# Routing tokens to experts by a table of token numbers and gates, and adding the experts' rows in DRAM

## The reference, cut to what matters

```python
x = layer_norm(DN_ALPHA * x + merged @ w_out[l], ln1_g[l], ln1_b[l])          # x1
gates = shared_group_router(xt, w_router, b_router)   # 2 of 16 experts, both in one group of 4
for e in range(N_EXPERTS):
    h = jax.nn.silu(xt @ w_gate[e]) * (xt @ w_up[e])                           # 1024 -> 512
    out = out + gates[:, e:e + 1] * (h @ w_down[e])                            # 512 -> 1024
x = layer_norm(DN_ALPHA * x + moe, ln2_g[l], ln2_b[l])
```

## Time and profile before

| what | us |
|---|---|
| median of 3 runs (lowest, highest) | 889.34 (886.75, 891.99) |
| the profiled execution | 887.89 |
| its span, first to last instruction | 886.4 |
| busy PE / DVE / ACT / POOL | 845.4 / 574.0 / 465.1 / 76.0 |
| weights of the experts, 96 loads of 1 MB, to landing (median) | 10.1 to 11.3 |

### The profile page before, as it was taken

How to read it: one execution, slowest core, us unless ns; L and a number is a source line. 1 busy time by engine, 2 the same in 40 slices (tenths; PEclk the granted TensorE clock), 3 DMA queues, 4 the chain that set the end, 5 groups by cost and what they waited for, 6 DMA issues and landing times.

```text
span 886.4 us, 12480 instructions
## 1 busy us (share of the span) xinstructions
PE 845.4 (95%) x4015; PEld 700.4 (79%) x4015; DVE 574.0 (65%) x623; ACT 465.1 (52%) x482; POOL 76.0 (9%) x137
## 2 busy tenths in 40 slices
PE   6999999979999999999999998899999999999993
PEld 5888788868888888888889988688888888888751
DVE  4777444333447884423445589478899889888727
ACT  3555433423466653323226541567787878778610
POOL 1100000400000000000000001301101110010040
PEclk9999999989999999999999998999999999999997
DMA  6565555873233334434329925699999999999753
GB/s 183 165 183 174 166 184 201 244 270 96 82 99 105 95 95 139 146 95 119 94 73 293 286 86 190 248 355 376 381 372 381 383 380 371 380 382 382 274 181 127
DMA packets 168096, 195.85 MB, mean 221 GB/s; under 512 B 7998, under 2 KB 106918, under 8 KB 168070
## 3 DMA queue, kind: packets, MB, share of 16 engines
q1 hardware_dynamic: 154374, 157.69, 53.4%
q0 software_dynamic: 10624, 32.57, 10.8%
q10 hardware_dynamic: 3072, 5.24, 1.6%
HBM read 164.94 MB, written 30.54 MB: 221 GB/s over the span
## 4 chain that ended last, share of the span: by engine, by line
PE 83%; DVE 6%; DMA 6%; ACT 2%; issue 1%; POOL 1%; SPq 0%; ACTq 0%; DVEq 0%; POOLq 0%
PE psA L554 7%; PE psA L553 7%; PE psA L555 7%; PE psA L722 6%; PE psA L723 6%; PE psA L724 6%; PE psB L553 6%; PE psB L555 6%; PE psB L554 6%; PE psB L743 3%; PE psB L745 3%; PE psB L744 3%; DMA wst<-in_w_out_dram 2%; DMA wst<-in_w_in_dram 2%; PE psD L553 2%; PE psD L555 2%
## 5 line engine op out<-in xcount | busy, mean ns | idle before, releaser
L1289 DVE TENSOR_TENSOR elo<-est,ehi 128x2048 fp32r<-128x2048 f32 x94 | 211.3, 2288 | 36.1 <-ACT ehi L971 36.0
L971 ACT ACTIVATE ehi<-est 128x2048 fp32r<-128x2048 f32 x92 | 173.3, 1914 | 35.7 <-DMA est<-in_w_exp_down_dram 14.9
L1102 DVE TENSOR_TENSOR wlo<-wst,whi 128x1024 fp32r<-128x1024 f32 (+1 forms) x78 | 97.5, 1249 | 96.8 <-ACT whi L818 95.7
L818 ACT ACTIVATE whi<-wst 128x1024 fp32r<-128x1024 f32 (+1 forms) x78 | 84.0, 1077 | 92.8 <-PE psA L555 36.4
L722 PE MATMUL psA<-ehi,xe_hi 128*128 128x512 f32 x256 | 101.7, 397 | 1.9 <-DVE xe_lo L1482 1.9
L723 PE MATMUL psA<-elo,xe_hi 128*128 128x512 f32 x256 | 100.5, 392 | 0.0
L724 PE MATMUL psA<-ehi,xe_lo 128*128 128x512 f32 x256 | 100.4, 392 | 0.0
L553 PE MATMUL psB<-xT_hi,whi 128*128 128x512 f32 x208 | 80.9, 389 | 0.0
L554 PE MATMUL psB<-xT_lo,whi 128*128 128x512 f32 x208 | 80.9, 389 | 0.0
L555 PE MATMUL psB<-xT_hi,wlo 128*128 128x512 f32 x208 | 80.9, 389 | 0.0
L722 PEld LDWEIGHTS psA<-ehi,xe_hi 128*128 128x128 f32 x256 | 48.5, 189 | 12.2 <-DVE xe_lo L1482 2.5
(11 more groups left out here) (277 smaller groups left out, 1613.5 us busy)
## 6 DMA issues: line engine op xcount, KB each, us to landing
est<-in_w_exp_gate_dram SPq DMA_DIRECT2D x32, 1024.0 KB, 11.3
est<-in_w_exp_up_dram SPq DMA_DIRECT2D x32, 1024.0 KB, 10.1
est<-in_w_exp_down_dram SPq DMA_DIRECT2D x32, 1024.0 KB, 10.9
wst<-in_w_in_dram SPq DMA_DIRECT2D x60, 512.0 KB, 4.0
xs<-zero POOLq DMA_DIRECT2D x23, 512.0 KB, 3.1
wst<-in_w_out_dram SPq DMA_DIRECT2D x16, 512.0 KB, 5.4
wst<-in_w_branch_r_dram SPq DMA_DIRECT2D x8, 640.0 KB, 4.3
ys<-yb ACTq DMA_DIRECT2D x32, 160.0 KB, 5.1
```

Of the source, the lines that this page charges most:

```text
L818: A(whi[p][:, 0:K, :], wst[p][:, 0:K, :], ACT.Copy).then_inc(w_hi, 1)
L971: A(ehi[s][:], est[s][:], ACT.Copy).then_inc(gu_hi if s < 4 else d_hi, 1)
L1102: V.tensor_tensor(wlo[p][:, 0:K, :], wst[p][:, 0:K, :], whi[p][:, 0:K, :], ALU.subtract).then_inc(w_lo, 1)
L1289: V.tensor_tensor(elo[s][:], est[s][:], ehi[s][:], ALU.subtract).then_inc(gu_lo if s < 4 else d_lo, 1)
```

## The change

The rows are no longer copied to `xs` and `ys`. x1 is stored twice in DRAM: `x1d`, from which the experts' rows are fetched, and `acc`, to which their outputs are added; each has 128 trash rows behind its 512. A table `tab` has for each of the 23 x 128 slots the token number and the gate, divided by alpha; an empty slot has a trash row's number (a different one for each slot of a block) and gate 0.

- SP loads slots 0 and 1 of expert 1, stores x1 to `x1d` tile by tile as it is ready and then to `acc`, and only then loads slots 2 to 5; no load waits for rows any more.
- POOL makes small constants, and after weight tile 20 clears the table and the trash rows, in place of all zero stores.
- The token numbers of blocks 0 and 1 come from DVE comparisons and eight small bf16 matmuls (keys, `chosen_by`, `pick0`), and POOL gathers these two blocks as soon as x1 is stored. Then it scatters the table's 8-byte entries with eight indirect DMAs, loads the whole table to SBUF (`lists`), and gathers block b when block b - 2 is transposed, into two buffers. Numbers of trash rows are out of bounds for a gather and are skipped.
- ACT evacuates the outputs scaled by the table's gates, into two buffers, and issues no DMA. POOL adds all 128 rows of a block to `acc` by an indirect DMA with add, when the add before has landed.
- The gates are computed before `dest` is released; both are in the table.
- In the tail SP loads the four tiles of `acc` when all adds have landed, and the layer norm is taken from them, with epsilon divided by alpha squared. PE has no part in it.
- The turns of PE are unrolled by two, those of ACT completely.

```diff
...
-            for s in range(6):
-                if s == 5:
-                    sp.wait_ge(xe_landed, 32)
+            for s in range(2):
+                load_expert(sp, 1, s)
+            for t in range(TT):
+                sp.wait_ge(x1_done, t + 1)
+                sp.dma_start(x1d[t * P:(t + 1) * P, :], x1[:, t, :]).then_inc(x1_stored, 16)
+            for t in range(TT):
+                sp.dma_start(acc[t * P:(t + 1) * P, :], x1[:, t, :]).then_inc(acc_seeded, 16)
+            for s in range(2, 6):
                 load_expert(sp, 1, s)
...
+            sp.wait_ge(y_stored, (more + NE) * 16)
+            for t in range(TT):
+                sp.dma_start(xa[:, t, :], acc[t * P:(t + 1) * P, :]).then_inc(got[t], 16)
             for t in range(TT):
                 sp.wait_ge(out_ready, t + 1)
-                sp.dma_start(out2[t * P:(t + 1) * P, :], yg[:, 0, t, :]).then_inc(stored, 16)
+                sp.dma_start(out2[t * P:(t + 1) * P, :], xa[:, t, :]).then_inc(stored, 16)
...
-            with pool.Fori(0, BLOCKS) as b:
-                pool.wait_ge(tile_done, b + 1)
-                pool.dma_start(xs[ds(b * P, P), :], zero[:]).then_inc(zero_done, 16)
-            with pool.Fori(0, NE) as b:
-                pool.wait_ge(tile_done, b + (BLOCKS + 1 - NE))
-                pool.dma_start(ys[ds(b * P + HEAD, P - HEAD), :], zero[HEAD:P, :]).then_inc(zero_done, 16)
-            with pool.Fori(NE, BLOCKS) as b:
-                pool.dma_start(ys[ds(b * P, P), :], zero[:]).then_inc(zero_done, 16)
-            pool.wait_ge(zero_done, ZEROS)
...
+            pool.wait_ge(tile_done, 20)
+            pool.dma_start(tab.rearrange("(b p) w -> b p w", p=P), vacant[0:BLOCKS]).then_inc(tab_cleared, 16)
+            for dram in (acc, x1d):
+                pool.dma_start(dram[S:S + P, :], zero[:]).then_inc(trash_zeroed, 16)
...
+            def gather(b, idx, most=S - 1):
+                pool.indirect_dma_start(out=xe[b % 2][:], out_offset=None, in_=x1d,
+                                        in_offset=bass.IndirectOffsetOnAxis(ap=idx, axis=0),
+                                        bounds_check=most, oob_is_err=False).then_inc(xe_landed[b % 2], 16)
+
+            def scatter_add(b, idx):
+                pool.wait_ge(y_evac, b * 2 + 2)
+                if b > 0:
+                    pool.wait_ge(y_stored, b * 16)
+                pool.sem_inc(pool_step, 1)
+                pool.indirect_dma_start(out=acc, out_offset=bass.IndirectOffsetOnAxis(ap=idx, axis=0),
+                                        in_=yb[b % 2][:], in_offset=None, compute_op=ALU.add).then_inc(y_stored, 16)
+
+            pool.wait_ge(x1_stored, 16 * TT)
+            pool.wait_ge(pick_done, 1)
+            gather(0, pick0[:, 0:1])
+            pool.wait_ge(pick_done, 2)
+            gather(1, pick0[:, 1:2])
             pool.wait_ge(dest_done, 1)
-            for t in range(TT):
-                for n in range(2):
+            for n in range(2):
+                for t in range(TT):
                     pool.indirect_dma_start(
-                        out=xs, out_offset=bass.IndirectOffsetOnAxis(ap=dest[:, n, t:t + 1], axis=0),
-                        in_=x1[:, t, :], in_offset=None).then_inc(scat, 16)
+                        out=tab, out_offset=bass.IndirectOffsetOnAxis(ap=dest[:, n, t:t + 1], axis=0),
+                        in_=pick[:, n, t, :], in_offset=None).then_inc(scat, 16)
             pool.wait_ge(scat, 16 * 2 * TT)
...
+            pool.dma_start(lists[:], tab.rearrange("(b p) w -> p b w", p=P)).then_inc(lists_landed, 16)
+            pool.wait_ge(lists_landed, 16)
+            for b in range(2, NE):
+                pool.wait_ge(xe_t, b - 1)
+                gather(b, lists[:, b, 0:1].bitcast(U32))
+                if b == 2:
+                    pool.wait_ge(acc_seeded, 16 * TT)
+                if b >= 4:
+                    scatter_add(b - 4, lists[:, b - 4, 0:1].bitcast(U32))
+            for b in range(NE - 4, NE):
+                scatter_add(b, lists[:, b, 0:1].bitcast(U32))
...
-            pe.wait_ge(block0_done, 1)
-            for k in range(KD):
+            for e in range(2):
+                pe.wait_ge(by_done, e + 1)
                 for t in range(TT):
-                    mm = pe.matmul(psC[0][:, k // 4, (k % 4) * P:(k % 4 + 1) * P],
-                                   x1[:, t, k * P:(k + 1) * P], block0[:, t, :],
+                    mm = pe.matmul(psA[e][:, 0:2], chosen_by[:, e, t, :], tokid[:, t, :],
                                    start=(t == 0), stop=(t == TT - 1))
...
+            warm(14, psB[0])
+            rows_t(0, 0, xe_landed[0], 16)
+            warm(9, psB[0])
             gate_up(0, first=True)
...
-            def y_out(b, s, first=False):
+            def y_out(b, s):
                 act.wait_ge(d_used, b * 2 + (s + 1))
-                if not first:
-                    act.wait_ge(y_stored, b * 32)
-                    act.wait_ge(y_rest_stored, b * 32)
-                A(yb[:, s * DF:(s + 1) * DF], psB[s], ACT.Copy).then_inc(y_evac, 1)
...
+                if b < 2:
+                    act.wait_ge(lists_landed, 16)
+                else:
+                    act.wait_ge(y_stored, b * 16 - 16)
+                A(yb[b % 2][:, s * DF:(s + 1) * DF], psB[s], ACT.Copy,
+                  scale=lists[:, b, 1:2].bitcast(F32)).then_inc(y_evac, 1)
...
             def summed(t):
-                dve.wait_ge(sum_done, t + 1)
-                moments([pairs[t][:, h, :] for h in range(2)], t % 2)
-                variance(t % 2, 1, 2 * TT + 2 * t + 2)
+                dve.wait_ge(got[t], 16)
+                moments(_halves(xa[:, t, :], S), t % 2)
+                variance(t % 2, 1, 2 * TT + 2 * t + 2, LN_EPS / ALPHA ** 2)
...
```

More of the change, by code:

```diff
@@ L278, in trunk_moe @@
         d_used = sem("d_used")
-        xe_landed = sem("xe_landed")
+        xe_landed = [sem(f"xe_landed{p}") for p in range(2)]
+        more_landed = sem("more_landed")
         xe_t = sem("xe_t")
@@ L510, in _ @@
-            load_rows(1, first=True)
-            pool.wait_ge(plan_done, 2)
-            load_rows(2)
-            with pool.Fori(3, NE) as b:
-                load_rows(b)
-                store_rest(b - 3)
-            for b in range(NE - 3, NE):
-                store_rest(b)
+            pool.dma_start(lists[:], tab.rearrange("(b p) w -> p b w", p=P)).then_inc(lists_landed, 16)
[7 more added lines that the diff above has]
+                    scatter_add(b - 4, lists[:, b - 4, 0:1].bitcast(U32))
@@ L521, in _ @@
                 with pool.Fori(0, more) as i:
-                    load_rows(i + NE)
-                    store_rest(i + NE)
-            pool.wait_ge(all_stored, 1)
-            for t in range(TT):
-                for n in range(2):
-                    pool.indirect_dma_start(
-                        out=yg[:, n, t, :], out_offset=None, in_=ys,
-                        in_offset=bass.IndirectOffsetOnAxis(ap=dest[:, n, t:t + 1], axis=0)
-                    ).then_inc(got[t], 16)
+                    pool.wait_ge(y_stored, (i + NE) * 16)
+                    pool.wait_ge(xe_t, i + NE)
+                    pool.dma_start(cur[:], tab[ds(i * P + NE * P, P), :]).then_inc(cur_landed, 16)
+                    pool.wait_ge(cur_landed, i * 16 + 16)
+                    pool.sem_inc(pool_step, 1)
+                    pool.indirect_dma_start(out=xe[0][:], out_offset=None, in_=x1d,
+                                            in_offset=bass.IndirectOffsetOnAxis(ap=cur[:, 0:1].bitcast(U32), axis=0)
+                                            ).then_inc(more_landed, 16)
+                    pool.wait_ge(y_evac, i * 2 + (2 * NE + 2))
+                    pool.wait_ge(y_stored, (i + NE) * 16)
+                    pool.sem_inc(pool_step, 1)
+                    pool.indirect_dma_start(out=acc, out_offset=bass.IndirectOffsetOnAxis(ap=cur[:, 0:1].bitcast(U32),
+                                                                                          axis=0),
+                                            in_=yb[0][:], in_offset=None, compute_op=ALU.add).then_inc(y_stored, 16)
         @block.tensor
@@ L692, in _ @@
             pe.wait_ge(sel_done, 1)
-            pe.wait_ge(masks, 4)
+            pe.wait_ge(masks, 8)
             for t in range(TT):
@@ L1056, in turn @@
                         e_round(b, 4 + s)
-                        y_out(b - 1, s, first_prev)
+                        y_out(b - 1, s)
                 hidden_round(b, first)
             turn(0, prev=False, first=True)
-            turn(1, first_prev=True)
-            with act.Fori(2, NE - 1) as b:
+            for b in range(1, NE - 1):
                 turn(b)
@@ L1084, in _ @@
                     hidden_round(b)
-                    for s in range(2):
-                        y_out(b, s)
-            act.wait_ge(y_stored, (more + NE) * 32)
-            act.wait_ge(y_rest_stored, (more + NE) * 32)
-            A(stat[:, 40:41], stat[:, 30:31], ACT.Copy).then_inc(all_stored, 1)
```

(8 more changed lines are left out.)

185 lines of the change are left out of this document (79 added, 106 removed).

## The result

The changed kernel takes 895.41 us (median of 8 runs, 893.06 to 900.05) beside 889.50 us for the kernel before on the same chip: ratio 1.0075, 95% interval 1.0056 to 1.0093, 6 us slower. The prediction, 888.8 us and no change, was wrong.

What follows compares the result with a forecast made beforehand. PE was taken as the bound, busy 845.4 of 886.4 us, with DMA at 18.40 us a turn behind it; 887.89 - 7.5 - 2.6 - 6.5 + 16.1 = 887.4, by the median 888.8 us, no change; 8 in 10: 871 to 908.

Steps and rivals of the forecast that it cites:

- Zeros, -7.5: First part, 160 to 201 us: removing the zero-store burst ends the stall of ACT and PE, -7.5 us.
- Trash stores and clear at tile 20, 0: First part: table clear and two 512 KB stores cost 2.9 us of DMA, hidden by PE's 8 us of cover; 0.
- x1 stored twice, 0: Before the experts: 4.2 MB of stores ahead of four expert 1 loads, hidden before gate_up 1; 0.
- rival D: First part: trash stores at tile 20 hit a weight load, so the early stall stays, 896.3 us; chance 0.04.
- Block 0 and 1, -2.6: Start of experts: block 1's wait goes (-1.4), late start +0.6, half clock gone -1.8; -2.6 us, bounds 0 and -4.
- The table, "Taken as 0": Start of experts: gather 2, behind table stores and list load, lands at 579 to 584, PE needs it near 583; 0.
- rival C: Start of experts: slow table stores delay gather 2 to about 594, PE waits 11 us, half hidden; 894.3 us, chance 0.06.
- Each turn, 19.87 us and 16.1 us of stall: Expert turns: DMA needs 19.87 us, 2.18 over PE; fourteen turns, 30.5 less the lead of 14.4, stall PE 16.1 us.
- A (17.69 to the end): Expert turns: the add is as cheap as a store, no stall; 874.7 us by the median, chance 0.28.
- B (21): Expert turns: the add costs all three passes, 21.12 us a turn, stall 33.6; 906.4 us by the median, chance 0.20.
- The 64 rows: Expert turns: a gather moves only filled rows, 64 on the mean, 0.92 us; the add always 128 rows, 2.64 us.
- The tail, -6.5: After the last evacuation: scatter 15 lands at 854, DVE starts at 857.5 not 862.26, 1.67 us wait gone; -6.5 us.

Runs made afterwards that it cites:

- spread_zeros: The kernel before with its zero stores spread, one of xs and one of ys behind each of the first 23 tiles: 880.94 us, ratio 0.9915.
- three_picked: The changed kernel with block 2's rows picked by comparisons and matmuls like blocks 0 and 1, without the table: 891.29 us, ratio 1.0031.
- plain_store: The changed kernel with the scatter with add made a plain store, so the sum over the two experts is left out: 877.28 us, ratio 0.9855.
- half_adds: The changed kernel with the add taking only the first 64 partitions of each block, other rows missing: 876.33 us, ratio 0.9852.
- last_apart: The changed kernel with the last block stored without add to another region, not waiting for the scatter ahead: 892.11 us, ratio 1.0030.

## Why the prediction was wrong

- *Zeros, -7.5.* Right: the stall is gone, and the burst alone is worth 7.6 us (spread_zeros). The first part gave 9.2; the other 1.8 lie within what profiles of this part differ by (522.1 to 525.7).
- *Trash stores and clear at tile 20, 0, and x1 stored twice, 0.* Right; rival D is out. Nothing waits near 200, and block 0 and 1 start on time.
- *Block 0 and 1, -2.6.* The route is right and the size too small: -4.4. The half clock's 1.8 us went as said; beside them 2.6 came where 1.4 - 0.6 = 0.8 was forecast. The list was picked at 536.7, a good 1 us ahead of the 547.0 less 9.2 that I had estimated, which is 1.1 of the 1.8 us between them; the rest wasn't traced.
- *The table, "Taken as 0".* This step failed. It measured 6.2 us, 3.6 of waiting and 2.6 of half clock, of which some 4 reach the end (three_picked). In the clock of the kernel before, which x1 reaches 9.2 us later, gather 2 landed at 585.3, where "579 to 584" stood, and PE ran dry at 581.8, where "near 583" stood. The issuing was right (stores 1.3 us apart, two slow ones) and the list load too (5.6 of 3 to 8). But the last store landed 6.9 us behind its issue, not the 3.9 of the earlier trace rows, gather 2 took 8.4 us to land where rival C reckons with 6.3, and a range that reached past the need was counted as nothing, with no half clock behind it. How late the rows come isn't fixed: other profiles of this head have waits of 1.2 to 6.4 us. Rival C had the mechanism, a late gather 2, and put it down to the issuing beside DVE, which was the smaller part.
- *Each turn, 19.87 us and 16.1 us of stall.* Right: turns of 19.7, and 16.9 us from block 4 to the last evacuation. The store with add costs 1.3 us more than the plain one; 1.32 was taken. By the row times above an add is 128 x 0.33 / 16 = 2.6 us, the 2.64 of the forecast. Rivals A (17.69 to the end) and B (21) are out. The Trainium skill's page "Collectives: The Full Stack", section on the bandwidth ceiling, says that an add needs a second source read, which halves the rate, and this trace agrees: 0.33 us of an engine for a row that is added against 0.16 for one that is stored. What I hadn't seen is what closes the loop: the slot's own landing plus the 4.5 us of split and reissue. A landing of 13.2 us is the longest that a turn of 17.69 bears; the earlier trace rows was at 13.5 already, and at 15.2 the turn is 19.7. In between the slot's loop is longer than PE's turn and the lead is spent: in the chains of plain_store and half_adds it takes 18.6 us in the mean (702.67 to 795.92 in five rounds, 703.88 to 778.20 in four) while most turns are still 17.7. The forecast's formula gives 18.61 for the plain store.
- *The 64 rows.* I charged 128 rows for the add and 64 for the gather, by bytes spread over all engines. Skipped rows leave the rest on half of the engines, the case that the prediction names for the gather alone (1.32, its dear end). With 1.32 its sum is 20.25 us a turn, more than the 19.7 measured, and the gather changes a turn by only 0.16 us between 64 and 128 rows. So the number 19.87 holds, but how the 0.92 for the gather enters it isn't shown.
- *The tail, -6.5.* This step failed too: -3.9 came. The 1.67 us wait went as said. But the last evacuation to the statistics took 12.07 us, not 9.45: POOL waited until 2.1 us behind the evacuation for add 14 (0.3 taken), though PE was starved, since this add, the first behind the last weight loads, landed 7.5 us from its issue (in the median of all 16 it is 10.0); and an add alone lands in 6.3 us, not 5.6. last_apart gets 4.0 us back.

By the steps: forecast -7.5 - 2.6 + 0 + 16.1 - 6.5 = -0.5; measured -9.2 - 4.4 + 6.2 + 16.9 - 3.9 (and 0.4 left over) = +6.0. The first two steps gained 3.5 us more than forecast, the stall cost 0.8 more, and the two that failed lost 6.2 and 2.6.

## What to carry to other kernels

Where transfers run beside weight loads that fill the DMA engines, price a turn as the landing time of one slot's load plus its way back to reissue, and put each byte moved twice (an add in DRAM) into that landing, for the engine that carries most rows and not for the mean of all. Skipping rows helps only if the rest lie on all engines. Plain stores to two slots and a sum on PE at the end, with block 2 picked ahead, were 18 us faster here. A table built by chained small transfers costs its landings, one after the other (6.9 and 4.1 us), so let the first blocks that it could delay go another way. And look whether stores that nobody waits for come in a burst: spreading them was worth 7.6 us in the kernel before, more than the difference between the two kernels.

## What the runs showed of the hardware that wasn't expected

An indirect transfer of 128 rows whose upper half is skipped by a bound runs on half of the 16 engines (51.2% of their time with nothing else under way, against 98.4% with all rows), and stays there when the list is reordered so that the filled rows lie in groups of four partitions out of every eight (48.5%). As an add it lands no sooner than a full one (6.21 and 6.32 us), while one of 64 places lands in 4.51. POOL needs longer to issue the store with add than the plain one: 2.4 us against 1.8 in the median, and 1.54 against 0.96 at the end, where nothing runs beside it. Alone, 512 KB in 128 rows land in 3.32 us as a store and in 6.32 as an add.
